# Two transformer layers of two kinds in one launch: the turned rows of each norm alternate with the first products, in banks of their own, and the next layer's first weight units are loaded a layer ahead

## The reference, cut to what matters

```python
h = rms_norm(x, norm_mix[i]) * (1.0 + sc1) + sh1        # D_MODEL 1024, 512 tokens (+ 256 context tokens in the first block)
hc = rms_norm(xc, norm_mix[i]) * (1.0 + sc1c) + sh1c
y, yc = token_mixers(h, hc, w_in[i], w_out[i], ...)
x = x + g1 * y
h = rms_norm(x, norm_ffn[i]) * (1.0 + sc2) + sh2
x = x + g2 * swiglu(h, w_gate[i], w_up[i], w_down[i])   # (silu(h @ w_gate) * (h @ w_up)) @ w_down
...
sh1, sc1, g1, sh2, sc2, g2 = jnp.split(s_lat @ w_mod[i] + b_mod[i], 6)
```

## Time and profile before

| | us |
|---|---|
| median of 3 runs | 3928.68 |
| lowest and highest | 3926.0 and 3930.54 |
| the profiled execution, its own time | 3924.18 |
| its span in the profile | 3922.4 |
| PE busy | 3509.7 |
| PEld busy | 2887.3 |
| DVE busy | 1784.7 |
| ACT busy | 1068.0 |

### The profile page before, as it was taken

The page is one execution under the profiler, slowest core; times in us unless marked ns, Lnnn a source line. Parts: engine busy times, 40 slices in busy tenths (PEclk is TensorE's granted clock), DMA queues, the critical chain, the costliest instruction groups (busy, mean ns, idle before and its releaser), DMA issues. The chain is left out here.

```text
span 3922.4 us, 49050 instructions
## 1 busy us (share of the span) xinstructions
PE 3509.7 (89%) x20368; PEld 2887.3 (74%) x20368; DVE 1784.7 (45%) x3354; ACT 1068.0 (27%) x1738; POOL 10.7 (0%) x12
## 2 busy tenths in 40 slices
PE   6998998999998988999998984799998983799997
PEld 4987777888886976878876962467887872568886
DVE  3225655333334235643445447653333448654333
ACT  2112443111113222532223222532222322532222
POOL 0000000000000000000000000000000000000000
PEclk9997999999999987999999985899999996799998
DMA  5340102423241210135543310026443320013332
GB/s 190 124 154 2 47 22 65 127 86 108 94 128 34 83 59 26 33 119 168 152 132 102 94 55 0 1 73 186 136 142 109 100 81 0 1 43 91 97 97 70
DMA packets 318717, 336.52 MB, mean 86 GB/s; under 512 B 12024, under 2 KB 233760, under 8 KB 318496
## 3 DMA queue, kind: packets, MB, share of 16 engines
q1 hardware_dynamic: 318496, 333.38, 27.7%
HBM read 329.67 MB, written 3.67 MB: 85 GB/s over the span
## 5 line engine op out<-in xcount | busy, mean ns | idle before, releaser
L1435 DVE TENSOR_TENSOR weights_low<-weights,weights_high 128x1024 fp32r<-128x1024 f32 (+4 forms) x424 | 485.8, 1148 | 1246.7 <-ACT weights_high L1073 1244.3
L1073 ACT ACTIVATE weights_high<-weights 128x1024 fp32r<-128x1024 f32 (+4 forms) x424 | 422.1, 997 | 1429.0 <-PE banks L552 959.0
L958 PE MATMUL banks<-h_high,weights_high 128*128 128x512 f32 (+1 forms) x1760 | 659.1, 374 | 10.4 <-DVE h_low L1447 9.0
L958 PE MATMUL banks<-h_low,weights_high 128*128 128x512 f32 (+1 forms) x1760 | 649.9, 369 | 0.0
L958 PE MATMUL banks<-h_high,weights_low 128*128 128x512 f32 (+1 forms) x1760 | 648.8, 369 | 0.0
L552 PE MATMUL banks<-weights_high,h_high 128*128 128x426 f32 (+3 forms) x1424 | 518.7, 364 | 2.7 <-DVE h_low L1447 2.7
L552 PE MATMUL banks<-weights_high,h_low 128*128 128x426 f32 (+3 forms) x1424 | 509.6, 358 | 0.0
L552 PE MATMUL banks<-weights_low,h_high 128*128 128x426 f32 (+3 forms) x1424 | 509.1, 357 | 0.0
L958 PEld LDWEIGHTS banks<-h_high,weights_high 128*128 128x128 f32 x1760 | 332.9, 189 | 84.6 <-DVE h_low L1447 16.6
L958 PEld LDWEIGHTS banks<-h_high,weights_low 128*128 128x128 f32 x1760 | 333.0, 189 | 55.8
L958 PEld LDWEIGHTS banks<-h_low,weights_high 128*128 128x128 f32 x1760 | 333.2, 189 | 51.9
(11 more groups left out here) (256 smaller groups left out, 3970.1 us busy)
## 6 DMA issues: line engine op xcount, KB each, us to landing
projected<-in_w_mod SPq DMA_DIRECT2D x80, 1024.0 KB, 5.3
weights<-in_w_gate_up SPq DMA_DIRECT2D x88, 512.0 KB, 3.9
weights<-in_w_down SPq DMA_DIRECT2D x80, 512.0 KB, 3.7
weights<-in_w_in SPq DMA_DIRECT2D x80, 426.0 KB, 3.4
weights<-in_w_gate SPq DMA_DIRECT2D x44, 512.0 KB, 6.6
weights<-in_w_up SPq DMA_DIRECT2D x44, 512.0 KB, 7.7
weights<-in_w_mod SPq DMA_DIRECT2D x32, 512.0 KB, 3.9
weights<-in_w_out SPq DMA_DIRECT2D x32, 512.0 KB, 3.7
```

Of the source, the lines that this page charges most:

```text
L958: mm = pe.matmul(bank[:, 0:cnt], wt[:, k, :], x[:, k, a:a + cnt], start=(k == 0 and q == 0), stop=(k == KD - 1 and q == 2))
L1073: act.activation(WH[s_ % 2][:, 0:k * n], slots[j % LAND][:, 0:k * n], ACT.Copy).then_inc(S["w_high"], 1)
L1435: dve.tensor_tensor(WL[s_ % 2][:, 0:k * n], slots[split_of[s_] % LAND][:, 0:k * n], WH[s_ % 2][:, 0:k * n].bitcast(F32), ALU.subtract).the ...
```

## The change

There are three parts, and some moves that follow from them.

1. **First norm** (layers 1 to 3; layer 0 keeps the old order). Four f are turned ahead of the product, into banks 4 to 7 with a semaphore of their own (`norm_banks`), and two more after each of the first two units. ScalarE and VectorE modulate f 4 and 5 behind their split of unit 2 and f 6 and 7 behind their split of unit 3. `warm(3)` is gone; `warm(4)` becomes `warm(5)` in layer 2 and nothing in layers 1 and 3. The small gate products move from the slots 0, 1, 6, 7 to 4, 5, 10, 11.
2. **Second norm** (all layers). `first_block` turns the first four f (two where there are two spans), then takes U0 and U1 together: for each f, three matmuls of U0 and three of U1 for each span, then the turning of one more f. The last two f are left for the end. TensorE's order with the tiles of `w_mod` was U0, tile 0, U1, tile 1, U2, tile 2, U3, tile 3, U4, U5, tile 4. It becomes U0 with U1, tile 0, U2, tile 1, U3, tile 2, U4, tile 3, U5, tile 4. SyncE's order of loads stays.
3. **Loads ahead.** At its end SyncE loads the following layer's first four `w_in` units and waits for them ahead of the barrier, and TensorE does `warm(8)` there.

```diff
+    early_units = []
+    if following:
+        n = W2 // 8 if following["second"] else 428
+        early_units = [(slots[i][:, 0:2 * n].rearrange("p (k n) -> p k n", n=n),
+                        following["w"]["w_in"][:, 0:n].rearrange("(k p) n -> p k n", p=PT)[:, 2 * i:2 * i + 2]) for i in range(LAND)]
+    def free_for_norm(B):
+        return [(len(B.past) + 4 + i) % 8 for i in range(4)]
+    def norm_banks(which, free):
+        return Banks([PS[i] for i in free], "turned%d" % which, S, {"d": "normed_low%d" % which})
...
         if not nxt:
             return []
-        if m < 2:
-            return [2 * m + "ad".index(by)]
-        return [m + 2] if by == "d" else []
+        if by == "a":
+            return [2 * m - 1] if m in (1, 2) else []
+        return [2 * m if m < 3 else m + 2]
...
-            there = turn_norm(0)
-            warm(3)
+            there = {}
+            if start_loads:
...
+            else:
+                if not squares:
+                    warm(5)
+                wait_normed(0, IN_T)
+                turned0 = norm_banks(0, range(4, 8))
+                for f in range(4):
+                    there[f] = turn_norm(turned0, IN_T, f)
+            def turn_beside(slot):
+                if not start_loads and slot < 2:
+                    for f in (4 + 2 * slot, 5 + 2 * slot):
+                        there[f] = turn_norm(turned0, IN_T, f)
...
-            there = turn_norm(1)
+            warm(14 if second else 10)
+            wait_normed(1, OUT_T)
+            def first_block():
+                free = free_for_norm(B)
+                T1 = norm_banks(1, free)
...
+                ahead = 4 // len(spans(OUT_T))
+                for f in range(ahead):
+                    there[f] = turn_norm(T1, OUT_T, f)
+                both = [(next_unit(later), [B.fill(pe, by) for _ in spans(OUT_T)]) for later, by in enumerate("ad")]
+                for k in range(KD):
+                    pe.wait_ge(S["normed_low1"], there[k])
+                    for (wh, wl), banks_ in both:
+                        for bank, (a, cnt, r) in zip(banks_, spans(OUT_T)):
+                            if k < KD - 2:
+                                gate_up(bank, wh, wl, a, cnt, [k])
+                    if k + ahead < KD:
+                        there[k + ahead] = turn_norm(T1, OUT_T, k + ahead)
...
+                        gate_up(bank, wh, wl, a, cnt, range(KD - 2, KD)).then_inc(S["filled"], 1)
...
+                    if m == 0:
+                        first_block()
+                        ready[m] = B.emptied_by("d")
+                        for i in mods_of(m, "d"):
+                            mod_beside(i)
+                        continue
...
+            if following:
+                warm(8)
...
+                elif not start_loads:
+                    continue
                 sp.dma_start(dst, src).then_inc(S["landed%d" % (j % LAND)], 16)
...
+            for i, (dst, src) in enumerate(early_units):
+                unit_free(sp, max(j for j in range(len(weight_units)) if j % LAND == i))
+                sp.dma_start(dst, src).then_inc(S["early"], 16)
+            if early_units:
+                sp.wait_ge(S["early"], 16 * LAND)
...
                     if (j, i) not in ((0, 0), (len(chunks) - 1, 3)):
                         split()
+                    if not start_loads and (j, i) in ((0, 1), (0, 2)):
+                        modulate(0, IN_T, turned0, (2 + 2 * i, 3 + 2 * i))
+                        if i == 2:
+                            all_modulated()
```

More of the change, by code:

```diff
@@ L534, in part_used, with product @@
                 release.append(("unit_part", mine["part"]))
-            def product(ah, al, tt, off, n, k0, k1, by, ready=None, B=B, after=None, behind=None):
+            def product(ah, al, tt, off, n, k0, k1, by, ready=None, B=B, after=None, behind=None, low="emptied_dve"):
                 out_banks = {}
@@ L561, in product, with wait_normed, turn_norm @@
                         after(k // 2)
[L563 to L567, removed]
+            def wait_normed(which, tt):
                 pe.wait_ge(S["normed%d" % which], (len(tt) + 1) // 2)
                 pe.wait_ge(S["normed_act%d" % which], len(tt) // 2)
[L570 to L577, removed]
+            def turn_norm(T, tt, f):
+                for a, cnt, r in spans(tt):
+                    bank = T.fill(pe, "d")
+                    for i in range(cnt // PT):
+                        mm = pe.transpose(bank[:, i * PT:(i + 1) * PT], XNV[:, a // PT + i, f * PT:(f + 1) * PT], ident)
+                    mm.then_inc(T.filled, 1)
+                return T.emptied_by("d")
             def turn_columns(src, by, tt=None):
@@ L933, in _, with gate_up @@
                 product(HH, HL, OUT_T, (0, 0), 512, 0, KD, lambda i: "d", None if j else there)
-            there = turn_norm(1)
+            warm(14 if second else 10)
+            wait_normed(1, OUT_T)
+            def gate_up(bank, wh, wl, a, cnt, kk):
+                for k in kk:
+                    for q, (wt, x) in enumerate(((wh, HH), (wh, HL), (wl, HH))):
+                        mm = pe.matmul(bank[:, 0:cnt], wt[:, k, :], x[:, k, a:a + cnt],
+                                       start=(k == 0 and q == 0), stop=(k == KD - 1 and q == 2))
+                return mm
+            def first_block():
+                free = free_for_norm(B)
+                T1 = norm_banks(1, free)
+                for i in free:
+                    B.free(pe, i)
+                there = {}
+                ahead = 4 // len(spans(OUT_T))
[10 more added lines that the diff above has]
+                        there[k + ahead] = turn_norm(T1, OUT_T, k + ahead)
+                done = B.filled_so_far() - 2 * len(spans(OUT_T))
+                for (wh, wl), banks_ in both:
+                    for bank, (a, cnt, r) in zip(banks_, spans(OUT_T)):
+                        gate_up(bank, wh, wl, a, cnt, range(KD - 2, KD)).then_inc(S["filled"], 1)
+                    done += len(spans(OUT_T))
+                    release.append(("filled", done))
+                T1.all_emptied(pe)
             def mod_beside(i):
@@ L1069, in split @@
                 _, _, (k, n), _ = weight_units[j]
-                act.wait_ge(S["landed%d" % (j % LAND)], 16 * (j // LAND + 1))
+                landed(act, j)
                 if s_ >= 2:
```

111 lines of the change are left out of this document (63 added, 48 removed).

## The result

The changed kernel's median is 3940.64 us (3933.38 to 3947.96, 9 runs), that of the kernel before 3929.1 (3925.71 to 3933.28, 9 runs). The ratio is 1.0028, with a 95% interval of 1.0018 to 1.0039: 0.28% or 11.5 us slower. Measured once more, it gave 3940.55 and 1.0035 (1.0021 to 1.0049). The range, 3917 to 3941, holds the time, but only just, by 0.4 us. The forecast, 3930.4 and a change within 0.2%, does not: the kernel is slower by more than that.

What follows compares the result with a forecast made beforehand. TensorE was taken as the bound, with time to win only where it waits or runs at half clock. Terms 5.2 - 2.8 - 3.2 + 0 + 0.2 + 0.9 - 0.5 - 1.5 = -1.7 gave 3930.4 us, range 3917 to 3941.

Steps and rivals of the forecast that it cites:

- the sum: Whole kernel: gains and losses of all places added up, 1.7 us slower than before.
- The block of U0 and U1: Second norm, layer 1: the first two units taken together end without waits, tile 0 done at 1735.6, gain 3.1 us.
- The waits of U2 to U6: Second norm, layer 1: TensorE waits for late splits and loads, 0.5, 2.2, 0.5, 2.2 and 0.5, 5.9 us in all.
- The wait for the fifth unit: First norm, layer 1: fifth `w_in` load waits for `h_ready`, so TensorE waits 3.6 us, leaving a gain of 0.2.
- The barrier: Layer ends: `warm(8)` takes 7.0 us, hidden in layers 0 and 2, and costs 1.5 in layer 1.
- The start of layer 2: First norm, layer 2: eight transposes behind each of the first two units, a gain of 0.9 us.
- Layer 0: Second norm, layer 0: the joint block ends earlier, with waits for `h_low` at each f, gain 5.2 us.
- Layer 3: Second norm comes out at 0; first norm, with no `warm` ahead, loses 0.5 us.
- Half clock: Rival: first two units of first norms in layers 1 to 3 at 1.2 GHz, about +12 us: 3942; chance 0.16.
- The weights come in time: Rival: waits at U3 to U6 vanish in layers 1 and 2, 10.8 us less: 3919.6; chance 0.24.

Runs made afterwards that it cites:

- the second norm's part alone: The kernel before with only the second norm's part of the change; first norm, its loads and barrier as before: 3936.7 us against 3928.11, ratio 1.0019.
- the small loads later: Changed kernel with the five small loads of layer 1's start moved behind the eighth unit: 3935.72 us, 1.0015 of before.
- three moves: Changed kernel with tile loads one unit later, layer 1's small loads behind the eighth unit, no `warm(8)` in layer 1: 3917.07 us against before's 3930.46, 0.997.
- the load order: Changed kernel with SyncE's loads of tiles 1 to 4 moved behind one more unit's load: 3928.32 us, 0.9997 of before.
- the loads alone: The kernel before plus only the loads ahead of the barrier and `warm(8)` at layer ends; both norms' orders as before: 3926.23 us against 3928.77, 0.9999.

## Why the forecast was wrong in its size and right in its steps

The mechanisms were those of the forecast; some sizes were not, and most of what they are off is one thing, the clock behind a wait. The changed places of the first profile lost 8.1 where the sum had 1.7. Behind waits, four units took longer than before, each from its first row to the end of its last: 1.4 (U3 of layer 1), 2.1 (the fifth unit of `w_in`), 1.1 and 2.2 (the first units of layers 2 and 3), 6.8 together. The sum had half clock at none of these.

1. **The block of U0 and U1** (gain of 3.1 in layer 1): right. Tile 0 came at 1733.43, and with the loads in time the stage gained 2.4 to 2.7 in layer 1 (forecast 2.6) and 3.0 to 3.1 in layer 2 (2.2).
2. **The waits of U2 to U6** (5.9 us in all): right in layer 1 as waits, 0.53, 2.69 + 0.17 and 2.87, together 6.3. *The term that was too small is what a wait costs.* I priced it by its length. Behind it TensorE can fall to half clock: 1.4 us more for U3 in the first profile, 1.6 and 2.9 for U3 and U5 in the second. So layer 1 lost 4.6 and 6.7, not 2.8; a slower U3 also takes up the 0.5 that U4 was to wait. In the four profiles that left both the loads and the waits as they were (the changed kernel's two, the second norm's part alone, the small loads later), U3 in layer 1 took 7.1 to 7.3; where the wait was filled it took 5.8 and 6.0. In layer 2 the clock fell in one of these four profiles. In the first it stayed up: the waits there were 0.50, 2.08, 0.41, 2.06 and 0.57, and the stage lost 2.5 where 3.2 was forecast. Moving the loads took wait and half clock away, and that shows the price of both: 12.3 us in the whole kernel.
3. **The wait for the fifth unit** (3.6 forecast): 5.00 measured (with layer 1's start 1.7 earlier taken off, TensorE was done 0.5 sooner than forecast and the unit there 0.9 later), and 2.1 more for the unit at half clock behind it. So the first norm of layer 1 lost 3.0 to 3.8 where I had a gain of 0.2. Without the wait it gained 3.9 in one profile and 3.2 in another (three moves); the forecast had said 3.8.
4. **The barrier**: 1.5 forecast, and the final norm's first instruction came 1.5 later behind layer 1's end (1.7 by the start of layer 2). The start of layer 2 was forecast to gain 0.9 and lost 0.7; its first unit, 5.2 us before, took 6.3 behind a wait of 2.94 for `h_low`. In all nine profiles with the new first norm it took 6.3 to 6.5, and in all five without it 5.2, so here the price doesn't vary. I had looked for half clock at a first unit in layer 1 only.
5. **Layer 0**: 5.2 forecast, 4.7 and 5.4 measured, in part by luck. The waits are not at each f; they are one of 2.86 ahead of the last two, with half clock behind it. U3 did wait, 1.09, and U5 0.55, where I had no wait. Against that, the first f, which I had at half clock, ran at full clock in the first profile (1.00 from 649.4 on). With the load order it did run at half clock (0.50 from 646 to 650), and the block took 28.4 us and not 25.9: so the stage gained 4.0 there, and 6.4 and 6.5 in two kernels whose block took 26.0.
6. **Layer 3** was forecast to lose 0.5 and lost 0.3, by two errors: its first unit took 7.4 at half clock, 5.2 before, and all the rest of its two norms gained 1.9. In the second profile the clock stayed up at that unit and the layer gained 2.2.

The step that failed is that the sum prices every wait of TensorE at its length. It rests on the sentence in *Half clock*: "Against: at layer 1's second norm TensorE waited 0.49 us in every 1.45 and the next three matmuls still took 0.96". The row is right, and waits of 0.5 us cost nothing but themselves here too. It says nothing on longer waits, and the sum had five, four of 2.2 and one of 3.6. The case of half clock, with 3942, had been given 0.16. Its mechanism is what happened, though in part at other places than the ones I named for it: behind the waits for loads, not only at the first units. That its 3942 lies so near to 3940.64 is luck: it is made of four units at 4 us each, and in the two profiles of the changed kernel no first unit took more than 2.2 longer, and no second unit ran slower. As for the section "A second HAM failure mode: psum-queue depth-cycling" of the Trainium skill's "TensorE: Matmul & The Clock Gate": the trace agrees with it that idle stretches between groups of matmuls cost throughput beyond their length (8.6 us for a unit of 5.7), but the short ones at the second norm of the kernel before, 0.49 us, did not show it; those behind loads did.

*The weights come in time*, the rival with 0.24, was worth 10.8 by the forecast. The load order made it true, and gave 12.3.

**What stays open.** Unchanged code takes up to 11.7 us more in the profiles of the changed kernels. The row of a mixer's small matmuls in layer 3, of before and of the kernel with the load order:

```profile
3356.10 1.55 PE L704 MATMUL banks<-projected,scratch 128*128 128x64 f32 x12
```

```profile
3360.05 2.82 PE L748 MATMUL banks<-projected,scratch 128*128 128x64 f32 x12
```

The same 12 rows take 1.3 us more, at the lower clock (granted 0.50 from 3360 to 3363, against 1.00 from 3356 to 3358 before). Before, the mixer has such groups at half clock too, but with the load order it has three more. Over the whole mixer the granted clock is 0.73 and not 0.75, and it takes 6.2 us longer. In the two profiles of before and in that of the loads alone the mixers differ by under 1 us; in the others a layer's mixer takes from 2.4 less to 6.2 more. Those three executions are at the low end of their kernels' times, and before's median lies some 4 to 6 above its profiles. So it isn't shown that the change brings this on, nor that it doesn't; the sum of the changed places alone, 8.1 and 8.5, leaves 3 us of the 11.5 to it. Why the same wait, of 2.1 or of 2.9 us, lowers the clock in one execution and not in another isn't settled either.

## What to carry to other kernels

When work is reordered on one engine, look whether the queue that loads for it needs the same shift: here a load that waits for a tile's use stood in front of the weights wanted next, and moving it by one unit turned the second norm's part from 0.19% slower into 0.32% faster (3917.95 against 3930.46). Price a wait on TensorE at its length plus what half clock behind it may cost: here 0 to 2.9 us more behind each wait of 2 to 3 us in front of a unit. And try each part of a change alone: the loads ahead and the first norm's part gave no gain that the medians show, in any combination tried.

## What was not expected of the hardware

- One wait of 2.87 us left a unit of 24 matmuls at 5.7 us, and one of 2.86 at the same place of the same kernel made it 8.6 (granted clock 1.00 and 0.50). Waits of 0.5 to 0.9 us between such units left the clock alone. Where only two to four transposes stood between waits of 0.3 to 2.0 us, the clock fell to 0.50 even behind constants multiplied at full clock.
- The multiplied constants are nearly four times as dear as the matmuls with rounded numbers of the same shape: 0.87 us against 0.23 for 512 columns (12.18 us for 14, at granted clock 1.00).
- Two profiles of the same kernel before agreed within 0.4 us at each of 64 marks, while its runs spread over 12 us.
